# A two-layer decoder trunk: group variance in a two-operand form, UV cleared in two halves, first group norm in smaller steps and transposed ahead of U3

## The reference

```python
def step(S, inp):
    r_t, d_t, k_t, v_t, aa_t, bb_t = inp
    sa = jnp.einsum('bhvk,bhk->bhv', S, aa_t)
    S = S * d_t[:, :, None, :] + sa[..., :, None] * bb_t[..., None, :] + v_t[..., :, None] * k_t[..., None, :]
    y = jnp.einsum('bhvk,bhk->bhv', S, r_t)
    return S, y
_, y = lax.scan(step, S0, xs)
mean = jnp.mean(y, axis=-1, keepdims=True)
var = jnp.mean(jnp.square(y - mean), axis=-1, keepdims=True)
y = ((y - mean) * lax.rsqrt(var + RWKV_GN_EPS)).reshape(B, T, D)
y = y * gn_w + gn_b
y = y + bonus.reshape(B, T, D)
return ((y * g) @ wo)
```

## Time and profile before

| | |
|---|---|
| Median of 3 executions | 1587.26 us (1586.25 to 1589.8) |
| Profiled execution, span from first to last instruction | 1587.1 us |
| TensorE busy | 1563.2 us, 98% |
| VectorE, ScalarE, GpSimd busy | 1226.4, 973.8, 68.4 us |
| TensorE, 177.3 to 196.5 us | 15.42 busy of 19.20 |
| Granted TensorE clock, 177.3 to 196.5 us | 1.00 |

### The profile page before, as it was taken

The page is one execution under the profiler, slowest core; times in us unless marked ns, Lnnn a source line. Parts: engine busy times, 40 slices in busy tenths (PEclk is TensorE's granted clock), DMA queues, the critical chain, the costliest instruction groups (busy, mean ns, idle before and its releaser), DMA issues.

```text
span 1587.1 us, 24869 instructions
## 1 busy us (share of the span) xinstructions
PE 1563.2 (98%) x9653; PEld 1299.0 (82%) x9653; DVE 1226.4 (77%) x980; ACT 973.8 (61%) x815; POOL 68.4 (4%) x35
## 2 busy tenths in 40 slices
PE   9999899999999999999999999999999999999997
PEld 7778858888998888888888888888888888888885
DVE  7573657774764457989988988988988988988995
ACT  1522345554424456787777777777777777777774
POOL 0013600000000000020000000000000000000100
PEclk9999999999999999999999999999999999999999
DMA  9120269956445524999999999999999999999991
GB/s 316 62 86 23 83 240 356 338 186 227 160 170 189 202 113 176 401 416 381 403 390 357 395 403 349 391 400 351 389 390 359 393 387 360 397 386 358 403 412 66
DMA packets 78588, 470.75 MB, mean 297 GB/s; under 512 B 7860, under 2 KB 8244, under 8 KB 26932
## 3 DMA queue, kind: packets, MB, share of 16 engines
q1 hardware_dynamic: 67860, 442.13, 72.3%
q10 hardware_dynamic: 9504, 23.37, 3.9%
q0 software_dynamic: 1152, 4.19, 0.7%
HBM read 450.27 MB, written 19.40 MB: 296 GB/s over the span
## 4 chain that ended last, share of the span: by engine, by line
PE 96%; DVE 2%; ACT 1%; issue 1%; DMA 0%; DVEq 0%; SPq 0%; ACTq 0%
PE ps L1641 93%; PE ps L2219 2%; PE ps L2211 0%; DMA h<-x 0%; PE ps L1660 0%; DVE workr L1057 0%; PE ps L1879 0%; ACT work L887 0%; DVE work L1375 0%; DVE h L1615 0%; DVE small L1194 0%; ACT workr L725 0%; ACT pairs_r L732 0%; PE ps L1948 0%; PE ps L2082 0%
## 5 line engine op out<-in xcount | busy, mean ns | idle before, releaser
L1641 PE MATMUL ps<-pairs_r,workr 128*128 128x512 f32 x2856 | 661.8, 390 | 0.6 <-DVE workr L1383 0.6
L1641 PEld LDWEIGHTS ps<-pairs_r,workr 128*128 128x128 f32 x2856 | 534.8, 188 | 112.4 <-issue 1.1
L1641 PE MATMUL ps<-workr 128*128 128x512 f32 x2024 | 483.6, 393 | 0.0
L1641 PEld LDWEIGHTS ps<-workr 128*128 128x128 f32 x2024 | 375.6, 188 | 77.4 <-DVE workr L1610 0.4
L1547 DVE TENSOR_TENSOR workr<-ring,workr 128x2048 fp32r<-128x2048 f32 x167 | 380.6, 2289 | 51.7 <-ACT workr L969 51.6
L1547 DVE TENSOR_TENSOR pairs_r<-ring,pairs_r 128x2048 fp32r<-128x2048 f32 x165 | 373.9, 2288 | 19.3 <-ACT pairs_r L969 17.3
L969 ACT ACTIVATE pairs_r<-ring 128x2048 fp32r<-128x2048 f32 x165 | 316.6, 1920 | 111.1 <-PE ps L1641 101.9
L969 ACT ACTIVATE workr<-ring 128x2048 fp32r<-128x2048 f32 x167 | 319.2, 1917 | 42.4 <-PE ps L1641 35.7
L1094 DVE TENSOR_TENSOR pairs_r<-ring,pairs_r 128x2048 fp32r<-128x2048 f32 x68 | 155.8, 2291 | 110.5 <-ACT pairs_r L732 109.1
L1641 PE MATMUL ps<-mem 64*64 64x64 f32 (+6 forms) x3064 | 198.9, 263 | 9.6 <-issue 4.1
L732 ACT ACTIVATE pairs_r<-ring 128x2048 fp32r<-128x2048 f32 x65 | 124.4, 1914 | 124.7 <-PE ps L1641 121.6
(11 more groups left out here) (231 smaller groups left out, 646.3 us busy)
## 6 DMA issues: line engine op xcount, KB each, us to landing
ring<-mstream SPq DMA_DIRECT2D x336, 1024.0 KB, 7.2
ring<-pstream SPq DMA_DIRECT2D x65, 1024.0 KB, 4.9
mem<-rstream SPq DMA_DIRECT2D x27, 512.0 KB, 8.4
sent<-work ACTq DMA_DIRECT2D x6, 1024.0 KB, 8.3
back<-work ACTq DMA_DIRECT2D x6, 1024.0 KB, 11.7
mem<-rstream SPq DMA_DIRECT2D x16, 256.0 KB, 2.9
work<-sent ACTq DMA_DIRECT2D x7, 512.0 KB, 7.9
back<-work ACTq DMA_DIRECT2D x7, 512.0 KB, 9.2
```

Of the source, the lines that this page charges most:

```text
L1641: ins = nc.tensor.matmul(*args, **kw)
```

## The change

Five things are edited. The scaling of the group variance becomes a scalar_tensor_tensor whose second operand is a column of epsilons in SBUF, broadcast; GpSimd fills that column at the start. The clearing of UV is cut in two: block 12 behind the K projection, block 13 behind the third part of AR. The first group norm has four steps: the reciprocal root comes after H1.6, the product after U2, the add after S2, and ScalarE's square root after X2. G0 moves ahead of U3, P1 behind it, and a new entry O0 runs the first tile of quarter 0 ahead of Y1. `ygT` moves to block 4, since P1 now reads AR after G0's store.

```diff
-        ygT = fm(blk(16))
+        ygT = fm(blk(4))
...
+        gneps = small[:, 186:187]
...
-                   W1.5:2 U1:0 P0:3 Q2.1:1 Y0:3 Q3.1:2 H1.5:0 S1:1 I2:3 X2:3 H1.6:2 Q3.0:0 U2:1 I3:3 S2:2 X3:3 P1:0
-                   U3:1 G0:2 Y1:0 G1:1"""
+                   W1.5:2 U1:0 P0:3 Q2.1:1 Y0:3 Q3.1:2 H1.5:0 S1:1 I2:3 X2:3 H1.6:2 Q3.0:0 U2:1 I3:3 S2:2 X3:3 G0:2
+                   U3:1 P1:0 O0:2 Y1:0 G1:1"""
...
-        jobs = [j for j in sequence if j[0] not in "IP"]
+        jobs = [j for j in sequence if j[0] not in "IPO"]
...
-        gn_after = {number["S", 1, 0]: (1,), number["U", 2, 0]: (2,), number["S", 2, 0]: (3,)}
-        gn_root_after = number["U", 2, 0]
+        gn_after = {number["S", 1, 0]: (1,), number["H", 1, LEVELS]: (2,), number["U", 2, 0]: (3,), number["S", 2, 0]: (4,)}
+        gn_root_after = number["X", 2, 0]
...
             nc.gpsimd.memset(uP[:, :, 0:1], 0.0).then_inc(s_pad, 1)
+            nc.gpsimd.memset(gneps, GN_EPS).then_inc(s_pad, 1)
+            pool.wait_ge(s_pj, J_K + 4)
+            nc.gpsimd.memset(blk(12), 0.0).then_inc(s_pz, 1)
             pool.wait_ge(s_pj, J_T1 + 1)
             link(nc.gpsimd.memset(restart, 1.0))
             nc.gpsimd.memset(restart.rearrange("p (c t) -> p c t", t=CH)[:, :, 0:1], 0.0).then_inc(s_rs, 1)
-            pool.wait_ge(s_g, 1)
-            nc.gpsimd.memset(blk(12, 2), 0.0).then_inc(s_pz, 1)
             pool.wait_ge(s_q, 48)
+            pool.wait_ge(s_AR, 3)
+            nc.gpsimd.memset(blk(13), 0.0).then_inc(s_pz, 1)
...
-            pool.wait_ge(s_pz, 1)
+            pool.wait_ge(s_pz, 2)
...
-            v.wait_ge(s_pad, 1)
+            v.wait_ge(s_pad, 2)
...
-                V.tensor_scalar(gvar, gvar, 1.0 / HN, GN_EPS, ALU.mult, ALU.add).then_inc(s_gv, 1)
+                V.scalar_tensor_tensor(out=gvar, in0=gvar, scalar=1.0 / HN, in1=gneps.to_broadcast([P, NH]), op0=ALU.mult,
+                                       op1=ALU.add).then_inc(s_gv, 1)
...
-                else:
+                elif step == 3:
                     v.wait_ge(s_gr0, 1)
                     v.wait_ge(s_gg0, 1)
+                    V.tensor_tensor(y[:, 8:16], y[:, 8:16], bc(gsd0)[:, 8:16], ALU.mult).then_inc(s_gh0, 1)
+                else:
                     yf = y.rearrange("p h v -> p (h v)")
-                    link(V.tensor_tensor(y[:, 8:16], y[:, 8:16], bc(gsd0)[:, 8:16], ALU.mult))
+                    v.wait_ge(s_gh0, 1)
                     v.wait_ge(s_cb, 2)
...
+                if kind == "O":
+
+                    wait_stored(("G", 0, 0))
+                    mixer_output(0, tiles=range(1))
+                    continue
                 if j == ("G", 1, 0):
 
-                    pe.wait_ge(s_ygT, 2)
-                    wait_stored(("G", 0, 0))
-                    mixer_output(0)
+                    mixer_output(0, tiles=range(1, KT))
```

More of the change, by code:

```diff
@@ L351, in build @@
         s_gg0 = sem("first_group_gated")
+        s_gh0 = sem("first_group_half_scaled")
         s_gg1 = sem("second_group_gated")
```

## The result

The changed kernel takes **1590.97 us** (median of 22 runs, 1586.95 to 1595.79). The kernel before, run beside it, takes 1588.34 us (22 runs, 1585.99 to 1592.6). The ratio is **1.0015, interval 1.0008 to 1.0022**: slower by 0.15%, about 2.4 us, within the 0.2% that I had called no change, but above my range.

A forecast was written before the change was run, and what follows sets the result against it. TensorE, busy for 98% of the 1587.1 us span, was taken as the bound; 0.69 us of standstill added and 0.89 removed gave net 0.20 less, 1587.26 to 1587.1 us (chance 0.62), range 1584.9 to 1588.6.

The forecast's parts named there:

- my range: Whole kernel: measured time expected between 1584.9 and 1588.6 us, with chance 0.94.
- the upper bound that I took: VectorE's variance scaling: held until GpSimd's L662 ends, 2.31 us as before, so 0 us gained by the two-operand form.
- The first rival: Variance on VectorE: new form not held, U2 waits 0.3 instead of 1.91, 1.6 us less, 1585.6 us; chance 0.25.
- The second: Slower rival at G0 ahead of U3: add held again, G0 waits, U3 0.5 to 0.65 later, 1587.7 us; chance 0.10.
- as costed: Clearing of UV: 3.34 us leave VectorE's queue at 81, M0 gains 0 to 0.33 us, 0 taken.
- their cover: Scalings L1136 at 41: may be held until 45.5, hidden by other ScalarE work and the gate's first projection; cost 0.
- 0.69 added, 0.89 removed, net 0.20 us less: TensorE's edited order: 0.69 us new standstill ahead of I3, 0.89 ahead of U3 gone, span 1587.1 to 1586.9.
- so the sum reaches the end whole: Behind G1: the weights of the next block move as one piece, so the 0.20 us gain arrives at the end.
- a standstill that I do not see: Anywhere on TensorE: an unseen wait making the kernel measurably slower, by 0.2% or 3.2 us; chance 0.03.
- 0.16 above the span that I count from: Whole kernel: median of earlier runs, 1587.26 us, taken as 0.16 above the profiled span of 1587.1.

The follow-up runs named there:

- the kernel with the hold lifted: The change with GpSimd's product made to wait until VectorE's scaling of the variance is written: ratio to the kernel before 0.9993, 1586.41 us.
- filled: The change with matmuls of zeros in TensorE's standstills: nine ahead of U2, 1.0005 (1587.99 us); with three more ahead of I3, 1.0005 (1589.22 us).
- root back: The change with reciprocal root and square root back behind U2 on their engines, G0 still ahead of U3: ratio to the kernel before 1.0004, 1588.72 us.
- again: The change, unaltered, run a second time on the chip of other follow-up runs: ratio to the kernel before 1.0009, 1590.40 us.
- clearing undone: The change with UV cleared in one go where it was, in place of the two halves: ratio to the kernel before 1.0016, 1592.44 us.
- root alone: The kernel before with only the reciprocal root moved behind H1.6 and the square root behind X2: ratio to the kernel before 1.0025, 1591.81 us.
- the two kernels with the hold lifted: The change with GpSimd's product waiting for the variance, 0.9993; and that with the reciprocal root behind Q3.0's store instead of ahead of it, 0.9978 (1586.51 us).

## Why the prediction was wrong

**The waits were right.** The two-operand form is held: 2.32 us, the upper bound that I took. By the Trainium skill, GPSIMD Engine Reference, Key points, GpSimd contends with VectorE instructions that have two SBUF inputs; the 2.32 us and the 0.18 of the kernel with the hold lifted agree. From the variance's start to U2's start it is 4.40 us in the earlier trace rows (180.86 to 185.26) and 4.40 after (179.14 to 183.54). The first rival fell. The second did not come about either: G0 waited for nothing, and the add took 0.68. The clearing was worth nothing at TensorE, as costed: L1153, the former L1148, has no instruction over 348 ns, M0 loads at 98.20 with the same seam of 0.33, and the scalings at 41 are held for some 1.0 us (3.18 in all) behind their cover. The standstill ahead of I3 measured 0.89 where I had 0.69 (my own times give 0.78, from U2's end at 186.41 to 187.19). From U2's start to U3's I forecast 7.04 us (185.26 to 192.3). Measured are 8.39 (183.54 to 191.93), and 7.03 without the 1.36 by which I3 and S2 were stretched.

**The step that failed** is "0.69 added, 0.89 removed, net 0.20 us less". It prices each standstill at its own length alone, so that one taken out behind X3 pays for one put in behind U2. The granted clock was no term of it, though the stretch had 1.00 in the profile to lose. With it fell "so the sum reaches the end whole": by the traces most of the time was lost far behind, in the routing stage. In its place the runs showed that the moved root lowers the mean clock (0.9930 against 0.9966 with that edit alone, and 1.0025 in time), and that it does not where the hold is lifted. The mean clocks, with that of before on the same chip in square brackets where there is one:

| | U2's standstill as it was | filled | gone with the hold |
|---|---|---|---|
| root behind U2's store | 0.9963 (before, all sets), 0.9963 [0.9968] (root back) | not tried | not tried |
| root moved forward | 0.9944 (the change), 0.9947 [0.9961] (again), 0.9939 [0.9961] (clearing undone), 0.9930 [0.9966] (root alone) | 0.9960 [0.9968], 0.9958 [0.9966] | 0.9965 [0.9968], 0.9964 [0.9961] |

That it takes the long standstill ahead of U2 is not shown: the filled kernels can't be told from the change nor from before, and lifting the hold shifts all that follows as well.

The sum with that term: 0.9945 over the 34 runs of the change, 0.9963 before, so 0.0018, and at 1.07 to 1.49 us for each 0.001 that is 1.9 to 2.7 us. Some 0.2 us of waits go off, 0.2 to 0.3 come in outside the span (below): 1.9 to 2.8. Measured are 2.4 and, the second time, 1.4 us, which is below that. My 0.03 for "a standstill that I do not see" had the wrong form: the standstill was in my text, the clock was not.

**The anchor** failed as well, in "0.16 above the span that I count from". Every one of the 129 later runs of the kernel before took 1.80 to 1.92 us longer than its span. By that, the profiled execution of 1587.1 us was one of some 1589 us, and the 1587.26 of three runs was a low median (1588.34 over 22, and 1588.1 to 1590.0 in the four later sets). With that offset my forecast would have stood at 1588.7, inside the spread of both kernels, and the sign would still have been wrong.

**What stays open.** That the loss is clock, and that it comes with the moved root, is borne out by the sets of runs. The way from the one to the other is not settled. A second standstill behind the first is one reading: two traces of the change have the fall right behind it. But the change run again has both standstills and no fall there, the traces of the root alone, of the root back and of the kernel before have falls behind U2's standstill by itself, and the fall in the routing stage, which parts the traces best, is far from both and has no standstill ahead of it. A delay of 0.86 us went with no such fall in the change and one of 1.72 with a fall in the kernel before, but one to three traces of a kernel give no rate. How much of the loss falls at 183 and how much at 619 can be told for the traces, not for the other runs.

## What to carry to other kernels

Where TensorE is busy for nearly the whole span, a change of waits can also change the granted clock, even far behind the edit, so a sum of standstills near nothing leaves the sign open: read the granted clock by stretch over the whole span, and set the mean clock beside each time. A fall of the clock in one trace may come in the kernel before as often, so take several traces of both before you call it the cause. A short VectorE instruction held by a GpSimd product was freed by a wait on GpSimd's side, not by the other form of it, and then the store that TensorE waits for goes ahead of the next norm's steps (0.9978 here). Count the offset from span to time in the same executions, never from one execution to the median of others.

## What the runs showed of the hardware that I had not expected

- A fall to half the clock behind standstills of 2.1 to 2.3 us lengthened U2, I3 and S2 by some 1.3 us wherever it began (4.60 to 4.66 us, or 1.15 and 3.48, against 3.33). Whether it came differed between executions of one kernel with the same standstill: two traces of six for either kernel. In the traces of the two kernels with the hold lifted, whose standstills are under 1 us, it did not come in that stretch; two traces are too few to set that apart from chance.
- Filler matmuls in a wait were no guard: the seven of the routing stage took 3.06 instead of 1.86 us as the clock fell under them, and what stands behind them began 0.80 us later. TensorE had been busy for 2.00 of 2.00 us in the window ahead (616 to 618).
- The time outside the span was longer where GpSimd had more instructions (medians): 1.85 us for the kernel before (all sets) and for the moved root alone, 2.00 with the clearing in halves alone or without it in the change, 2.07 to 2.12 for the change, 2.14 with one wait more on GpSimd. Why is not shown.
